# Three weight conversions, two bound matmuls and one split product set at other places in a three-layer kernel

## The chip, the core and the metric

The kernel runs on one core of one Trainium2 chip. The engines are TensorE (PE), VectorE (DVE), ScalarE (ACT), GpSimd (POOL) and SyncE (SP, which here only issues DMAs). The metric is the device time of one execution in microseconds. Before the change the median of 3 runs is 2321.61 us (2321.58 to 2321.97).

## The reference

The input is one sequence of 512 tokens with 1024 channels, in float32. It goes through an HGRN2 layer and a chunk-banded attention layer, each with a SwiGLU part, and then through a block in which half of the channels go to a two-directional mLSTM and half to a two-directional Hyena convolution, followed by an MLP. What is touched lies in that last block:

```python
hn = rms_norm_2(x, norm_mix_pre)
proj = (hn @ w_in).astype(f32)
cv = short_conv3(proj[..., :N_CONV], conv_w.astype(f32), conv_b.astype(f32))
q = heads(jax.nn.silu(cv[..., OFF_MQ:OFF_MQ + M_WIDTH]))
k = heads(jax.nn.silu(cv[..., OFF_MK:OFF_MK + M_WIDTH])) * (M_HEAD_DIM ** -0.5)
v = heads(proj[..., OFF_MV:OFF_MV + M_WIDTH])
o_gate = jax.nn.sigmoid(proj[..., OFF_MO:OFF_MO + M_WIDTH])
...
h_fwd = mlstm_chunkwise(q, k, v, gates[:, 0], jax.nn.log_sigmoid(gates[:, 1]))
h_bwd = flip(mlstm_chunkwise(flip(q), flip(k), flip(v), flip(gates[:, 2]), ...))
...
z = cv[..., OFF_HV:OFF_HV + H_WIDTH]
z = cv[..., OFF_HX1:...] * two_sided_fft_conv(z, filt[:, 0, 0], filt[:, 1, 0], fb[0])
z = cv[..., OFF_HX2:...] * two_sided_fft_conv(z, filt[:, 0, 1], filt[:, 1, 1], fb[1])
```

The mLSTM has 4 heads of 128 channels and, in the kernel, is computed without chunks: the 512 x 512 matrix of weights of each head and direction, exp(-max(bound - column, 0)), times the scores of queries and keys.

## The kernel before, in words

**Precision and weights.** Almost every matmul is three matmuls, from a high and a low half of each operand (`three`, L679 to L682). Weights come in slots of 128 x 2048 floats by DMA into one of 3 `raw` buffers. ACT copies a slot to its high half, `w_hi` (L1373, in `feed`), and DVE subtracts to get its low half, `w_lo` (L1847, also in a `feed`). There are 2 such pairs, used in turn. ACT and DVE are each one queue that is run in the order in which the program is written, and each calls `ahead(label, i)` at chosen places: it converts every slot up to the one behind (label, i) that isn't converted yet. So a call that is taken away puts its slot to the next call behind it. PE waits at the head of a slot for its `w_lo` (`weights`).

**Gates and mqk.** PE works through the slots mgate, mqk 0 to 3 (queries and keys, two chunks of 128 channels each), mv 0 and 1 (values), mo 0 and 1 (output gates), h2 0 to 5. In the loop over the four slots of mqk, DVE scales PE's result out of its bank (`scaled_conv`, L2258), ACT takes the middle tap of the convolution (L1650), DVE the outer ones (L2272, L2273), ACT the SiLU (L1655). Into slot i = 1 of that loop the gates are put: DVE copies their rows (L2299, L2300) and takes absolute values (L2301, releases `mg_q`), ACT takes the exponential (L1671) and the logarithm (L1673, releases `mg_l`), and in i = 2 and 3 DVE computes running sums and running maxima (L2304 to L2313). The first slot of mv claims all four rotating banks, which the chunks before must have left.

**mLSTM.** For each head h and direction d, PE spreads the bound over the partitions (`bound`, L1121; heads 2 and 3 use bank 0), DVE takes the differences (`exponents`, L2329, releases `ml_a`), ACT the exponential (`weights_of`, L1679), POOL masks four diagonal blocks (`mask_of`, L636), PE computes the scores (L1166), DVE multiplies (`masked`, L2341, releases `ml_p`), PE multiplies by the values (L1187; first the forward direction, then the backward one, four matmuls each, of which each makes two instructions), POOL sums the blocks (L650 to L658), PE sums over partitions (L1203), DVE inverts (L2359 to L2361) and puts the result on diagonals (L1890), PE spreads it (L1209), DVE combines (L2368 to L2370). `fill(n)` puts n steps of the output gates' matmuls between.

**Hyena.** For each of two orders o, PE transforms forward by a cosine and a sine table (eight outputs, `FORWARD`), DVE multiplies the spectra in four frequency blocks f (six operations each, L2421 to L2427, into buffers that alternate by f), ACT takes the high halves of the product (`upper_product`, L1740), DVE the low ones (`lower_product`, two L1861 for each f, release `u_l`), and PE transforms back (`back`): four groups of three matmuls for each block k of the cosine part, k = 0, 1, 2, then k = 0, 1 of the sine part, then the rest. `back` of block k waits for the low half of product k.

## Time and profile before

| what | value |
|---|---|
| median of 3 runs | 2321.61 us |
| the profiled execution's own time | 2321.61 us |
| its span | 2319.6 us |
| its mean granted clock of TensorE | 0.975 of full speed |
| PE busy | 2189.9 us, 94% |
| DVE busy | 1410.4 us, 61% |
| ACT busy | 752.1 us, 32% |
| POOL busy | 424.3 us, 18% |

The span runs from the first to the last instruction of the profiled execution; its own time is 2.0 us more. A busy share counts the time in which an engine had at least one instruction at work; matmuls overlap, so a busy PE is not PE at its peak. In a timeline each row gives the start in microseconds from the span's beginning, the duration, the engine, the line of the kernel, the operation with its output and inputs, how many like it stand in a row, and in brackets how long the engine had been idle and who ended that.

### The profile page before, as it was taken

The numbers are of one execution on the slowest core, as the hardware profiler recorded it, in microseconds if no ns is written. First come the engines' busy times: TensorE is split into PE (matmuls) and PEld (weight loads), VectorE is DVE, ScalarE is ACT, GpSimd is POOL, SyncE is SP. The second block draws the span as 40 slices with busy tenths as digits, with TensorE's granted clock in tenths as the row PEclk, the third lists the DMA queues.
The fourth block names the chain that finished last, engine by engine and source line by source line (L and its number), as shares of the span: only waits on it lengthen the run. The fifth ranks groups of instructions, "written<-read, shape, count | busy, mean of one in ns | idle before, by whom it ended". The sixth has DMA issues, their size and how long they took to land.

```text
span 2319.6 us, 25720 instructions
## 1 busy us (share of the span) xinstructions
PE 2189.9 (94%) x10094; PEld 1752.1 (76%) x10094; DVE 1410.4 (61%) x1929; ACT 752.1 (32%) x961; POOL 424.3 (18%) x272
## 2 busy tenths in 40 slices
PE   7899999979999997999989999998999998999997
PEld 5588788767888886866678888876568876888885
DVE  5666766554767767177455444467565776655656
ACT  1443334332222223256432222244233333322321
POOL 0000000039998873200000000000420000000000
PEclk9999999989999998999999999999999998999998
DMA  6343231225555542422122322322112221323220
GB/s 245 124 161 109 92 127 57 71 84 188 200 182 182 182 163 94 143 91 74 52 76 91 99 101 91 109 94 69 41 48 98 92 81 65 109 91 109 91 91 37
DMA packets 39327, 249.54 MB, mean 108 GB/s; under 512 B 4627, under 2 KB 4819, under 8 KB 11112
## 3 DMA queue, kind: packets, MB, share of 16 engines
q1 hardware_dynamic: 32856, 230.97, 28.7%
q0 software_dynamic: 3008, 10.63, 1.4%
q10 hardware_dynamic: 3344, 6.29, 0.7%
q8 instruction: 82, 1.34, 0.2%
q14 instruction: 37, 0.30, 0.0%
HBM read 241.58 MB, written 6.29 MB: 107 GB/s over the span
## 4 chain that ended last, share of the span: by engine, by line
PE 81%; DVE 8%; issue 4%; POOL 3%; ACT 2%; DMA 1%; SPq 0%; ACTq 0%; DVEq 0%; POOLq 0%
PE bank L680 24%; PE bank L682 23%; PE bank L681 23%; PE bank L907 2%; DVE w_lo L1847 2%; PE bank L727 1%; ACT w_hi L1373 1%; PE bank L1025 1%; PE bank L1035 1%; PE bank L1046 1%; POOL raw L593 1%; PE bank L714 1%; DMA raw<-in_wts 1%; PE bank L823 1%; POOL raw L594 1%
## 5 line engine op out<-in xcount | busy, mean ns | idle before, releaser
L680 PE MATMUL bank<-u_hi,w_hi 128*128 128x512 f32 x1708 | 695.1, 407 | 40.3 <-DVE w_lo L1847 11.8
L682 PE MATMUL bank<-u_hi,w_lo 128*128 128x512 f32 x1708 | 672.9, 394 | 0.0
L681 PE MATMUL bank<-u_lo,w_hi 128*128 128x512 f32 x1708 | 672.8, 394 | 0.0
L1847 DVE TENSOR_TENSOR w_lo<-raw,w_hi 128x2048 fp32r<-128x2048 f32 x162 | 427.8, 2641 | 225.9 <-ACT w_hi L1373 225.8
L680 PEld LDWEIGHTS bank<-u_hi,w_hi 128*128 128x128 f32 x1708 | 325.8, 191 | 129.6 <-issue 49.0
L1373 ACT ACTIVATE w_hi<-raw 128x2048 fp32r<-128x2048 f32 x162 | 309.1, 1908 | 341.6 <-PE bank L682 300.4
L682 PEld LDWEIGHTS bank<-u_hi,w_lo 128*128 128x128 f32 x1708 | 325.0, 190 | 70.0
L681 PEld LDWEIGHTS bank<-u_lo,w_hi 128*128 128x128 f32 x1708 | 326.1, 191 | 67.0 <-issue 3.8
L680 PE MATMUL bank<-g_hi,w_hi 128*128 128x512 f32 x772 | 306.2, 397 | 13.8 <-DVE w_lo L1847 6.4
L681 PE MATMUL bank<-g_lo,w_hi 128*128 128x512 f32 x772 | 301.8, 391 | 0.0
L682 PE MATMUL bank<-g_hi,w_lo 128*128 128x512 f32 x772 | 301.7, 391 | 0.0
L593 POOL TENSOR_TENSOR raw<-raw,cact 128x2048 f32<-128x2048 f32 x36 | 132.8, 3690 | 556.3 <-DVE u_lo L1913 483.3
L1935 DVE SCALAR_TENSOR_TENSOR H<-bank,modc,H 128x512 f32<-128x512 f32 x192 | 138.3, 745 | 84.7 <-PE bank L682 83.8
L680 PEld LDWEIGHTS bank<-g_hi,w_hi 128*128 128x128 f32 x772 | 145.7, 189 | 53.3 <-DVE w_lo L1847 8.2
L682 PEld LDWEIGHTS bank<-g_hi,w_lo 128*128 128x128 f32 x772 | 145.6, 189 | 30.9
L681 PEld LDWEIGHTS bank<-g_lo,w_hi 128*128 128x128 f32 x772 | 145.8, 189 | 29.0
L1549 ACT ACTIVATE pool<-bank 128x512 f32<-128x512 f32 x44 | 26.3, 599 | 314.8 <-PE bank L682 314.8
L594 POOL TENSOR_TENSOR raw<-raw 128x1024 f32<-128x1024 f32 x36 | 125.0, 3473 | 2.8
L2116 DVE TENSOR_TENSOR pool<-pool,bank 128x512 f32<-128x512 f32 x44 | 30.2, 687 | 154.8 <-ACT pool L1549 147.8
L1865 DVE TENSOR_TENSOR g_lo<-pool,g_hi 128x512 fp32r<-128x512 f32 x96 | 104.0, 1090 | 0.2
L2530 DVE TENSOR_TENSOR pool<-pool,bank 128x512 f32<-128x512 f32 x120 | 80.6, 684 | 23.6 <-PE bank L682 23.3
L626 POOL DMA_DIRECT2D pool<-in_tri x1 | 0.5, 536 | 453.2 <-DVE H L1935 453.2
(284 smaller groups left out, 2262.0 us busy)
## 6 DMA issues: line engine op xcount, KB each, us to landing
raw<-in_wts SPq DMA_DIRECT2D x218, 1024.0 KB, 4.8
spectra<-pool ACTq DMA_DIRECT2D x16, 256.0 KB, 2.0
scr<-in_rel POOLq DMA_DIRECT2D x16, 256.0 KB, 3.4
pool<-spectra POOLq DMA_DIRECT2D x16, 256.0 KB, 3.0
H<-in_x ACTq DMA_DIRECT2D x1, 2048.0 KB, 21.3
out<-H SPq DMA_DIRECT2D x8, 256.0 KB, 2.0
pool<-in_window POOLq DMA_DIRECT2D x1, 1024.0 KB, 9.1
pool<-in_filt_w POOLq DMA_DIRECT2D x1, 512.0 KB, 6.2
```

Of the source, the lines that this page charges most:

```text
L593: link(pl.tensor_tensor(chunks, chunks, cact[:, :].unsqueeze(2).broadcast_to((P, KC, 256)), ALU.mult))
L594: link(pl.tensor_tensor(src[:, 0:1024], src[:, 0:1024], src[:, 1024:2048], ALU.add))
L680: pe.matmul(out, lh, rh, start=start, stop=False, skip_group_check=True)
L681: pe.matmul(out, lh, rl, start=False, stop=False, skip_group_check=True)
L682: return pe.matmul(out, ll, rh, start=False, stop=stop, skip_group_check=True)
L907: mm = pe.matmul(b[:, t * P:(t + 1) * P], k[:, t * P:(t + 1) * P], q[:, t * P:(t + 1) * P], start=True, stop=True)
L1373: act.activation(w_hi[RING[w]][:, :], raw[s % raw_ring][:, :], ACT.Copy).then_inc(hi_done, 1)
L1847: dve.tensor_tensor(w_lo[RING[w]][:, :], raw[W_STREAM[w] % raw_ring][:, :], w_hi[RING[w]][:, :].bitcast(F32), ALU.subtract).then_inc(lo_do ...
L1865: dve.tensor_tensor(g_lo[:, n % NG, :], src, g_hi[:, n % NG, :].bitcast(F32), ALU.subtract).then_inc(g_l, 1)
L1935: dve.scalar_tensor_tensor(H[:, c, :], b[:, :], mcol(gate, c), H[:, c, :], ALU.mult, ALU.add).then_inc(free["dve"], 1)
L2116: dve.tensor_tensor(ff_h[:, i % 2, :], ff_s[:, i % 2, :], read(n + 1)[:, :], ALU.mult).then_inc(free["dve"], 1)
L2530: dve.tensor_tensor(Facc[:, c, :], Facc[:, c, :], b[:, :], ALU.add).then_inc(free["dve"], 1)
```

## The change

It has five places. In the mLSTM, `bound(h+1, 1)` for heads 2 and 3, with its wait, goes from ahead of both directions of L1187 to between them. In the loop over mqk, `ahead("mqk", 2)` is taken out of i = 1 on ACT and on DVE, which leaves slot mqk 3 to the same call at the start of i = 2. On DVE `ahead("mo", 1)`, which converts the first slot of h2, goes from head 2, behind `masked(3)`, to the end of head 1's round. In the hyena part `lower_product(2)` goes from ahead of the operations of f = 3 to behind them.

```diff
--- before.py
+++ after.py
@@ -1171,15 +1171,15 @@
             head_scores(0)
             fill(2)
             for h in range(M_HEADS):
-                if 2 <= h + 1 < M_HEADS:
-                    pe.wait_ge(ml_a, 2 * (h + 1) + 1)
-                    bound(h + 1, 1)
                 pe.wait_ge(ml_p, 8 * (h + 1))
                 if h:
                     pe.wait_ge(ml_nev, 2 * h)
                 else:
                     pe.wait_ge(ml_a, 2)
                 for d in range(2):
+                    if d and 2 <= h + 1 < M_HEADS:
+                        pe.wait_ge(ml_a, 2 * (h + 1) + 1)
+                        bound(h + 1, 1)
                     order = range(TB) if d == 0 else range(TB - 1, -1, -1)
                     for i in order:
                         a, z = (i * P, SEQ) if d == 0 else (0, (i + 1) * P)
@@ -1666,7 +1666,6 @@
                     act.wait_ge(*free_of(FIRST["mgate"]))
                     act.activation(g_all, g_all, ACT.Identity, bias=vcol("b_gates")).then_inc(mg_b, 1)
                 if i == 1:
-                    ahead("mqk", 2)
                     act.wait_ge(mg_q, 1)
                     act.activation(gt[0:M_HEADS], gt[0:M_HEADS], ACT.Exp, scale=-1.0).then_inc(mg_e, 1)
                     act.wait_ge(mg_e, 1)
@@ -2293,7 +2292,6 @@
                 for c in (2 * i, 2 * i + 1):
                     update_H(c)
                 if i == 1:
-                    ahead("mqk", 2)
                     dve.wait_ge(mg_b, 1)
                     for d in range(2):
                         dve.tensor_copy(gi[0:M_HEADS, d, :], g_all[64 * d:64 * d + M_HEADS, :])
@@ -2353,8 +2351,6 @@
                 if h + 1 < M_HEADS:
                     masked(h + 1)
                     scaled_out(FIRST["mo"] + h, m_og[:, h, :])
-                if h == 2:
-                    ahead("mo", 1)
                 dve.wait_ge(ml_den, h + 1)
                 link(dve.tensor_tensor(m_dd[:, 0:8], bank[6][:, 0:8], em[:, :, h], ALU.max))
                 link(dve.scalar_tensor_tensor(m_dd[:, 0:8], bank[6][:, 0:8], -1.0, m_dd[:, 0:8], ALU.mult, ALU.max))
@@ -2370,6 +2366,8 @@
                 dve.tensor_tensor(m_h[:, h, :], m_h[:, h, :], scr[:, 3, :], ALU.add).then_inc(ml_h, 1)
                 if h + 2 < M_HEADS:
                     exponents(h + 2, 1)
+                if h == 1:
+                    ahead("mo", 1)
             scaled_out(FIRST["mo"] + M_HEADS - 1, m_og[:, M_HEADS - 1, :])
             ahead("h2", 0)
             dve.wait_ge(ml_h, M_HEADS)
@@ -2408,7 +2406,6 @@
                 for f in range(4):
                     e = 4 * o + f
                     if f == 3:
-                        lower_product(2)
                         ahead("dft", 2 * o + 1)
                     if f >= 2:
                         dve.wait_ge(u_l, U_Y[o] + 2 * (f - 1))
@@ -2431,7 +2428,7 @@
                         ins = dve.tensor_copy(ys[0:1, :], bb[0:1, :])
                     ins.then_inc(hy_y, 1)
                     dve.wait_ge(hy_y, e + 1)
-                    if f in (1, 2):
+                    if f:
                         lower_product(f - 1)
                 lower_product(3)
                 if o:
```

What this does to the queues is seen at three places. On ACT, in the loop over mqk, the high half of slot mqk 3 (L1373) stands ahead of the exponential and the logarithm of the gates (L1671, L1673) before:

```order
L1655 ACTIVATE pool<-pool 128x512 x2
L1373 ACTIVATE w_hi<-raw 128x2048
L1671 ACT_TABLE_LOAD
L1671 ACTIVATE scr<-scr 4x1024
L1673 ACT_TABLE_LOAD
L1673 ACTIVATE scr<-scr,onec 4x1024
L1650 ACTIVATE pool<-macc,vec 128x512 x2
L1655 ACT_TABLE_LOAD
```

and now (where those two are L1670 and L1672):

```order
L1655 ACTIVATE pool<-pool 128x512 x2
L1670 ACT_TABLE_LOAD
L1670 ACTIVATE scr<-scr 4x1024
L1672 ACT_TABLE_LOAD
L1672 ACTIVATE scr<-scr,onec 4x1024
L1373 ACTIVATE w_hi<-raw 128x2048
L1650 ACTIVATE pool<-macc,vec 128x512 x2
L1655 ACT_TABLE_LOAD
```

The same slot's low half moves in the same way on DVE, from ahead of the gate rows to behind them.

On DVE, in the mLSTM, from the last `exponents` (L2329) of head 3 over `masked(3)` (L2341) to the inversion (L2359), before:

```order
L2329 TENSOR_SCALAR pool<-bank,pool 128x512
L2341 SCALAR_TENSOR_TENSOR pool<-bank,pool 128x512
L2341 SCALAR_TENSOR_TENSOR pool<-bank,pool 128x128
L2341 SCALAR_TENSOR_TENSOR pool<-bank,pool 128x384
L2341 SCALAR_TENSOR_TENSOR pool<-bank,pool 128x256 x2
L2341 SCALAR_TENSOR_TENSOR pool<-bank,pool 128x384
L2341 SCALAR_TENSOR_TENSOR pool<-bank,pool 128x128
L2341 SCALAR_TENSOR_TENSOR pool<-bank,pool 128x512
L2258 TENSOR_TENSOR pool<-bank,macc 128x512
L1847 TENSOR_TENSOR w_lo<-raw,w_hi 128x2048
L2359 TENSOR_TENSOR pool<-bank,pool 128x8
L2360 SCALAR_TENSOR_TENSOR pool<-bank,pool 128x8
```

and now (`exponents` is L2327, `masked` L2339, the inversion L2355 and L2356, `w_lo` L1846):

```order
L2327 TENSOR_SCALAR pool<-bank,pool 128x512
L1846 TENSOR_TENSOR w_lo<-raw,w_hi 128x2048
L2339 SCALAR_TENSOR_TENSOR pool<-bank,pool 128x512
L2339 SCALAR_TENSOR_TENSOR pool<-bank,pool 128x128
L2339 SCALAR_TENSOR_TENSOR pool<-bank,pool 128x384
L2339 SCALAR_TENSOR_TENSOR pool<-bank,pool 128x256 x2
L2339 SCALAR_TENSOR_TENSOR pool<-bank,pool 128x384
L2339 SCALAR_TENSOR_TENSOR pool<-bank,pool 128x128
L2339 SCALAR_TENSOR_TENSOR pool<-bank,pool 128x512
L2257 TENSOR_TENSOR pool<-bank,macc 128x512
L2355 TENSOR_TENSOR pool<-bank,pool 128x8
L2356 SCALAR_TENSOR_TENSOR pool<-bank,pool 128x8
```

The conversion of h2's first slot has moved from behind the seven rows of `masked(3)` and the scaled gate to ahead of them.

On DVE, in the first hyena pass, the rows from the last of f = 2 to the last `lower_product` (L1861), before:

```order
L2427 TENSOR_TENSOR scr<-scr 128x512
L1861 TENSOR_TENSOR u_lo<-scr,u_hi 128x512 x4
L1847 TENSOR_TENSOR w_lo<-raw,w_hi 128x2048
L2421 TENSOR_TENSOR scr<-pool 128x512
L2422 TENSOR_TENSOR scr<-bank,pool 128x512
L2423 TENSOR_TENSOR scr<-pool 128x512
L2424 TENSOR_TENSOR scr<-bank,pool 128x512
L2426 TENSOR_TENSOR scr<-scr 128x512
L2427 TENSOR_TENSOR scr<-scr 128x512
L1861 TENSOR_TENSOR u_lo<-scr,u_hi 128x512 x2
```

and now (L1860, with the six operations as L2418 to L2424):

```order
L2424 TENSOR_TENSOR scr<-scr 128x512
L1860 TENSOR_TENSOR u_lo<-scr,u_hi 128x512 x2
L1846 TENSOR_TENSOR w_lo<-raw,w_hi 128x2048
L2418 TENSOR_TENSOR scr<-pool 128x512
L2419 TENSOR_TENSOR scr<-bank,pool 128x512
L2420 TENSOR_TENSOR scr<-pool 128x512
L2421 TENSOR_TENSOR scr<-bank,pool 128x512
L2423 TENSOR_TENSOR scr<-scr 128x512
L2424 TENSOR_TENSOR scr<-scr 128x512
L1860 TENSOR_TENSOR u_lo<-scr,u_hi 128x512 x4
```

Two of the four low halves ahead of `w_lo` now stand behind the six operations of f = 3. The second pass changes in the same way.

## Rows read from the trace of the kernel before

**Rows 1.** The page, part 1: engine, busy us, share of the span, instructions.

```profile
PE 2189.9 (94%) x10094; PEld 1752.1 (76%) x10094; DVE 1410.4 (61%) x1929; ACT 752.1 (32%) x961; POOL 424.3 (18%) x272
```

**Rows 2.** Timeline of PE (start, us, engine, line, operation, idle before), after four waits.

```profile
435.63 0.77 PE L680 MATMUL bank<-u_hi,w_hi 128*128 128x512 f32 x1 [3.23 <-DVE u_lo L1861]
...
1149.55 0.50 PE L680 MATMUL bank<-g_hi,w_hi 128*128 128x512 f32 x1 [2.92 <-DVE w_lo L1847]
...
1589.98 0.50 PE L680 MATMUL bank<-u_hi,w_hi 128*128 128x512 f32 x1 [1.70 <-DVE w_lo L1847]
...
1608.64 0.77 PE L680 MATMUL bank<-w_hi,u_hi 128*128 128x512 f32 x1 [7.44 <-DVE macc L2258]
```

**Rows 3.** Timeline of ACT, gates.

```profile
1585.70 1.90 ACT L1373 ACTIVATE w_hi<-raw 128x2048 fp32r<-128x2048 f32 x1
...
1595.22 1.15 ACT L1673 ACTIVATE scr<-scr,onec 4x1024 f32<-4x1024 f32 x1
```

**Rows 4.** Timeline of DVE, gates.

```profile
1587.63 2.29 DVE L1847 TENSOR_TENSOR w_lo<-raw,w_hi 128x2048 fp32r<-128x2048 f32 x1 [1.19 <-ACT w_hi L1373]
...
1591.59 1.21 DVE L2301 SCALAR_TENSOR_TENSOR scr<-scr 4x1024 f32<-4x1024 f32 x1
...
1597.17 0.75 DVE L2272 SCALAR_TENSOR_TENSOR pool<-macc,vec,pool 128x511 f32<-128x511 f32 x1 [3.17 <-ACT pool L1650]
...
1605.00 2.29 DVE L1847 TENSOR_TENSOR w_lo<-raw,w_hi 128x2048 fp32r<-128x2048 f32 x1
...
1607.21 1.28 DVE L2258 TENSOR_TENSOR macc<-bank,macc 128x512 f32<-128x512 f32 x2
```

**Rows 5.** Timeline of DVE, heads 2 and 3 of the mLSTM.

```profile
1687.68 1.91 DVE L2329 TENSOR_SCALAR pool<-bank,pool 128x128 f32<-128x128 f32 x4
...
1694.85 1.68 DVE L2341 SCALAR_TENSOR_TENSOR pool<-bank,pool 128x512 f32<-128x512 f32 x4 [5.25 <-POOL pool L636]
...
1699.90 2.28 DVE L1847 TENSOR_TENSOR w_lo<-raw,w_hi 128x2048 fp32r<-128x2048 f32 x1
...
1702.10 0.16 DVE L2359 TENSOR_TENSOR pool<-bank,pool 128x8 f32<-128x8 f32 x1
```

**Rows 6.** Timeline of DVE, both hyena passes.

```profile
1819.16 2.50 DVE L1861 TENSOR_TENSOR u_lo<-scr,u_hi 128x512 fp32r<-128x512 f32 x4
...
1827.49 0.69 DVE L2427 TENSOR_TENSOR scr<-scr 128x512 f32<-128x512 f32 x1
...
1871.51 0.68 DVE L2427 TENSOR_TENSOR scr<-scr 128x512 f32<-128x512 f32 x1
```

**Rows 7.** Timeline of PE, third input block of both backward passes.

```profile
1824.23 0.39 PE L680 MATMUL bank<-u_hi,w_hi 128*128 128x512 f32 x1
...
1868.23 0.39 PE L680 MATMUL bank<-u_hi,w_hi 128*128 128x512 f32 x1
```

**Rows 8.** Timeline of PE, heads 2 and 3.

```profile
1683.47 1.88 PE L1209 MATMUL bank<-scr,ones 128*128 128x512 f32 x4
...
1686.34 4.58 PE L1187 MATMUL bank<-pool 128*128 128x512 f32 x16
...
1698.99 1.84 PE L1203 MATMUL bank<-onec,scr 128*128 128x1 f32 x16
...
1703.90 2.26 PE L1209 MATMUL bank<-scr,ones 128*128 128x512 f32 x4 [0.19 <-DVE scr L1890]
```

**Rows 9.** Timeline of ACT and of POOL, head 3.

```profile
1690.81 1.90 ACT L1373 ACTIVATE w_hi<-raw 128x2048 fp32r<-128x2048 f32 x1
...
1693.11 1.71 POOL L636 TENSOR_TENSOR pool<-pool 128x128 f32<-128x128 f32 x4
```

**Rows 10.** Stretches of PE: from:to us, length, busy (instructions), granted clock, DMA share, GB/s.

```profile
435.60:441.00 5.40, 5.37 (x13) 0.50 0.01 3
...
1608.60:1612.00 3.40, 3.36 (x8) 0.50 0.64 270
```

**Rows 11.** The line L636 of POOL: count, ns least/median/most, first and last start.

```profile
L636 POOL TENSOR_TENSOR pool<-pool x32: 449/458/2512, 1628.6 to 1694.4; 128x128 f32<-128x128 f32 x32
```

## The prediction

> **What bounds the kernel now.** I read the busy shares first: PE is busy 94% of the span [rows 1], so a wait costs time only where PE has nothing else to issue, or where it ends last for PE. Then I read the timelines of PE, DVE, ACT and POOL at the three places that the diff touches, looking for PE's idle time and for what ended it.
>
> - The gates (1585 to 1622 us). PE stands 1.70 us before the last slot of mqk, for its w_lo, and 7.44 us before the first slot of mv, for DVE's L2258 (`scaled_conv` of channel 7, which frees a bank) [rows 2]. DVE is the late one there, and DVE waited 3.17 us for ACT, which was at the exponential and the logarithm [rows 3, 4].
> - The mLSTM heads (1640 to 1716 us). PE, DVE and POOL hand each head on; before head 3's `masked`, DVE stands 5.25 us until POOL's L636 [rows 5], and that is the chain.
> - The two hyena passes (1805 to 1885 us). PE streams without a gap, and DVE delivers the low halves just ahead of it [rows 6, 7].
>
> **The change, part by part.** Times are those of before; a later place is shifted by what the earlier ones add.
>
> *1. Bounds.* `bound(h+1,1)` for heads 2 and 3 goes behind the four forward matmuls of L1187, half of 4.58 us [rows 8], so about 2.2 us later; PE issues the same work, and its wait on ml_a was already met. DVE's exponents of (3,1) start about 0.9 us later than 1687.68, and ACT's w_hi behind them at 1691.7 instead of 1690.81 [rows 5, 9]. Alone this is hidden: in before w_hi is wanted only at 1699.90 [rows 5]. Alone I put it at 0, between -0.2 and +0.9 (what DVE loses, if something waited for it). With part 3 the 0.9 us is no longer covered.
>
> *2. The last slot of mqk.* ACT's w_hi and DVE's w_lo now stand behind the gate rows. DVE goes into them at 1586.4 (1.19 us idle before 1587.63 [rows 4]). They took from the end of w_lo, about 1589.9, to 1592.8 (1591.59 + 1.21), 2.9 us: now done at 1589.3. From there to the end of the logarithm it took 1596.37 - 1592.80 = 3.57 us [rows 3, 4]: now 1592.9. Then w_hi, 1.90 us [rows 3], to 1594.8, then w_lo, 2.29 us, to about 1597.1. PE starts the slot there instead of at 1589.98, standing 8.8 us instead of 1.70. Much is paid back. The slot took 11.2 us at full clock (1589.98 to 1608.64 - 7.44). After 8.8 us of rest the clock will be at its 1.2 GHz level, as it was after 7.44 us (granted 0.50 from 1608.6 to 1612 [rows 10]); the slow stretch costs half its length, 1.7 us there (3.4 us) and 2.7 us after a rest of 3.23 us (5.4 us [rows 2, 10]); I take 2.2, the middle. PE ends the slot at 1597.1 + 11.2 + 2.2 = 1610.5, L2258 of channel 7 follows in 0.7 us (two take 1.28 [rows 4]), and mv starts at 1611.2. The conversion for it is not late: DVE's taps start at 1597.1 + 1.28 for the two L2258 and some 0.4 for ACT's middle tap (my allowance), so at 1598.8 instead of 1597.17, and w_lo moves from 1605.00 to 1606.6 and ends by 1608.9 [rows 4]. Before, mv started at 1608.64 with a slow stretch of its own worth 1.7; now the rest is under 1 us and it runs at full clock. Net 1611.2 - (1608.64 + 1.7) = +0.9 us. Bounds: +0.4 and +1.4 with 1.7 and 2.7, and +2.6 if mv starts slow all the same.
>
> *3. The first slot of h2.* w_lo leaves the place before L2359 at head 2, where PE's column sums were done about 1700.8 and DVE came at 1702.10 [rows 5, 8]: at most 1.3 us of DVE. It goes ahead of `masked(3)`. ACT's w_hi ends at 1691.7 + 1.90 = 1693.6, and w_lo runs 1693.7 to about 1696.0; in before `masked(3)` began at 1694.85. Worse, POOL's four L636 of head 3 stand at 1693.11 to 1694.82 [rows 9], and `masked(3)` needs them. An L636 takes 0.46 us and in one case 2.51 [rows 11], the one that met a w_lo. So after two of them POOL stands until 1696.1, two more end at 1697.1, and `masked(3)` starts 2.3 us late. PE's column sums move from 1698.99 to 1701.3; four gate steps behind them fill 2.9 us, and L1209 comes at 1705.8 instead of 1703.90. Before, L1209 also waited between its pairs and ended at 1706.2 (2.26 us for four, where free ones take 1.88 [rows 8]); now 1705.8 + 1.9 = 1707.7. Net +1.5 us. Bounds: +2.3 if all of the delay is passed on, and -0.7 if w_lo were hidden (four gate steps after 1700.7 end at 1703.6, and 1703.6 + 1.9 stands against 1706.2); only DVE's own 1.1 us late gives +0.4.
>
> The Trainium skill, "SBUF — State Buffer", section on SBUF's two separate sides, says that the pair of ports shared by VectorE and GpSimd is locked for a whole instruction, so that the loser fully blocks. By that rule the late start is the full 2.3 us, without it 1.1; the trace agrees (2.51 us [rows 11]).
>
> *4. Hyena.* `lower_product(2)` goes behind the six operations of f = 3 in both passes. In before it was inside the four L1861 at 1819.16 [rows 6], and PE took up its third input block, the ninth group of three, at 1824.23 (1868.23 in the second pass) [rows 7], 2.6 us after. w_lo of the table gains nothing, since it waits for ACT's w_hi and starts at 1822.15 as before. So f = 3 ends when it did: 1827.49 + 0.69 = 1828.18, and 1871.51 + 0.68 = 1872.19 in the second pass [rows 6]. Then one L1861, 0.69 us, and PE's third block starts at 1828.95 and 1872.95, so PE stands 4.7 us per pass. It has nothing else to issue: `back` takes the blocks in order, and the groups behind it are queued. Nothing gives this back, because from here on PE ends last: DVE stood idle before the output rows of each pass. In stalls: 9.4 us. A rest of 4.7 us lies above the one of 3.23 us after which the clock was at its lower level, and above the 2.92 us after which it was not (first matmul 0.77 against 0.50) [rows 2]. So I take a fall in each pass, 2.2 us each (bounds 0 and 2.7). Sum 2 x (4.7 + 2.2) = 13.8; bounds 9.4 and 14.8.
>
> Sum: 0 + 0.9 + 1.5 + 13.8 = +16.2 us. The profiled execution took 2321.61 us with a span of 2319.6; its own time is the median of the three runs. So 2337.8 us, span 2335.8.
>
> **The rivals.**
>
> *B. The clock holds in the hyena stalls.* For it: the stall begins out of dense work, as the one of 2.92 us did; against it, the rest of 3.23 us. It gives 0.9 + 1.5 + 9.4 = +11.8, 2333.4 us; with a fall in one pass alone 2335.6. The Trainium skill, "TensorE: Matmul & The Clock Gate", Part 1, says that the chip's view of PE's activity runs free of the program, so that the point of change differs from run to run; by that a stall of this length can pass without a fall, which is this rival, 0.25.
>
> *C. The postponed product is not waited for*, because PE comes to the third block later than the trace shows. Then only parts 2 and 3 count, +2.4, 2324.0. Against it: both passes show PE there 4.7 us too early, and nothing moved shifts PE against DVE inside a pass. 0.04.
>
> *D. Faster.* The exponential and the logarithm start 1592.8 - 1589.3 = 3.5 us earlier, and the 7.44 us before mv hang on them. If PE got its mqk weights in time, mv would start 3.5 us earlier, -3.5. It decides only if ACT could convert between the exponential's wait and its start; in the new order w_hi stands behind the logarithm on ACT. It also needs C; with part 3's best case 2321.6 - 3.5 - 0.7 = 2317.4. 0.03.
>
> *E. More is lost*: mv starts slow (+1.7), all of part 3 is passed on (+0.8), and the slow stretches are long (+1.0): 2341.3. 0.08.
>
> **How the numbers follow.** The forecast, 2337.8 with its own range 2335 to 2340.5, gets 0.60, B 0.25, E 0.08, C 0.04, D 0.03. The range of 2331 to 2341.5 takes in B and E. A measurement of this kernel can tell 0.2% from no change, 4.6 us: forecast, B and E lie above it, 0.93; C is within, 0.04; D is 4.2 us faster, on the edge of it, and the chance of a gain beyond that is 0.03.
>
> **What would show it.** PE idle about 8.8 us before the last mqk slot and under 1 us before mv; two new waits of PE of 4.7 us for L1861 (now L1860) in the backward passes, each with granted clock at 0.5 behind it; `masked(3)` behind a w_lo, with one L636 over 2 us; the same instruction counts. It is wrong if PE does not wait in the backward passes, or if the total there is under 9 us; if the clock holds, the time falls by 2.2 us per pass.

## The result and the profile after

The changed kernel takes 2347.86 us (median of 4 runs, 2342.69 to 2348.81), the kernel before beside it 2321.6 us (2321.33 to 2321.97). The ratio is 1.0104, with an interval of 1.0090 to 1.0118: slower by 1.0%. The profiled execution took 2343.47 us with a span of 2341.5 and a mean granted clock of 0.969; before it was 2321.61 us and 0.975. So the traces show 21.9 us of the loss, and it is these that are taken apart here. Repeated on another occasion, the changed kernel had a median of 2342.96 us against 2322.84, ratio 1.0084 [1.0071, 1.0097]; both intervals hold 0.90 to 0.97%.

Timeline of PE, the gates, after (start, us, engine, line, operation, idle before), as in [rows 2]:

```profile
1597.23 0.79 PE L680 MATMUL bank<-u_hi,w_hi 128*128 128x512 f32 x1 [8.78 <-DVE w_lo L1846]
...
1611.69 0.47 PE L680 MATMUL bank<-w_hi,u_hi 128*128 128x512 f32 x1 [0.95 <-DVE macc L2257]
```

Timeline of ACT and DVE there, as in [rows 3, 4]:

```profile
1591.91 1.15 ACT L1672 ACTIVATE scr<-scr,onec 4x1024 f32<-4x1024 f32 x1
1592.96 1.89 ACT L1373 ACTIVATE w_hi<-raw 128x2048 fp32r<-128x2048 f32 x1
1594.89 2.29 DVE L1846 TENSOR_TENSOR w_lo<-raw,w_hi 128x2048 fp32r<-128x2048 f32 x1 [5.38 <-ACT w_hi L1373]
```

The wait has moved from in front of mv (7.44 us before) to in front of the last mqk slot (8.78 us, before 1.70). The two waits add up to 9.73 us where there were 9.14, and the exponential and the logarithm are indeed earlier, but `w_hi` has to stand behind them.

Timeline of POOL, DVE and PE at head 3, as in [rows 5, 8, 9]:

```profile
1694.58 3.76 POOL L636 TENSOR_TENSOR pool<-pool 128x128 f32<-128x128 f32 x4
```

```profile
1695.03 2.59 DVE L1846 TENSOR_TENSOR w_lo<-raw,w_hi 128x2048 fp32r<-128x2048 f32 x1 [3.14 <-ACT w_hi L1373]
1698.37 1.69 DVE L2339 SCALAR_TENSOR_TENSOR pool<-bank,pool 128x512 f32<-128x512 f32 x4 [0.76 <-POOL pool L636]
...
1706.97 0.17 DVE L2355 TENSOR_TENSOR pool<-bank,pool 128x8 f32<-128x8 f32 x1 [0.99 <-PE bank L1203]
```

```profile
1699.32 2.08 PE L1166 MATMUL bank<-pool 128*128 128x512 f32 x2 [3.92 <-DVE pool L2339]
1700.40 1.42 PE L680 MATMUL bank<-u_hi,w_hi 128*128 128x512 f32 x1
1701.62 0.63 PE L681 MATMUL bank<-u_lo,w_hi 128*128 128x512 f32 x1
```

POOL's four L636 take 3.76 us instead of 1.71 with `w_lo` running beside them, `masked(3)` starts behind them, and PE waits 3.92 us before the third L1166. The matmul behind it (L681) takes 0.63 us, which is what one takes at half clock; at full clock it is 0.39. Before, PE waited 1.75 us there and the matmul took 0.39 (timeline of PE, before):

```profile
1695.79 1.12 PE L1166 MATMUL bank<-pool 128*128 128x512 f32 x2 [1.75 <-DVE pool L2341]
...
1696.99 0.39 PE L681 MATMUL bank<-u_lo,w_hi 128*128 128x512 f32 x1
```

Timeline of PE and DVE in the hyena passes, as in [rows 6, 7]; the PE rows are the third input block of both passes:

```profile
1835.89 0.80 PE L680 MATMUL bank<-u_hi,w_hi 128*128 128x512 f32 x1 [4.57 <-DVE u_lo L1860]
...
1887.20 0.80 PE L680 MATMUL bank<-u_hi,w_hi 128*128 128x512 f32 x1 [4.58 <-DVE u_lo L1860]
```

```profile
1834.42 0.68 DVE L2424 TENSOR_TENSOR scr<-scr 128x512 f32<-128x512 f32 x1
1835.14 2.50 DVE L1860 TENSOR_TENSOR u_lo<-scr,u_hi 128x512 fp32r<-128x512 f32 x4
```

These two waits did not exist before: PE took the same block up without idle time [rows 7]. Stretches of all engines after (from:to, length, busy of each engine, granted clock, DMA share, GB/s), as in [rows 10]:

```profile
1835.90:1841.50 5.60, 5.60 (x14) 4.39 (x15) 1.74 (x3) 0.39 (x1) 0.57 (x2) 0.53 0.31 94
1887.20:1892.80 5.60, 5.60 (x14) 4.44 (x15) 4.16 (x7) 2.49 (x5) 0.00 (x0) 0.54 0.00 0
1699.30:1702.70 3.40, 3.38 (x6) 2.06 (x7) 1.65 (x4) 0.00 (x0) 0.00 (x0) 0.50 0.65 275
1736.00:1740.00 4.00, 4.00 (x14) 3.42 (x14) 3.31 (x7) 2.08 (x2) 0.00 (x0) 0.50 0.00 0
```

The clock is at its 1.2 GHz level behind both hyena waits, behind the wait of head 3, and once more 37 us later at 1736, where PE had not waited at all. The last stretch has a smaller fellow in the kernel before:

```profile
1732.00:1736.00 4.00, 4.00 (x13) 0.64 0.00 0
```

### The profile page after: what moved, and what is told of

The parts are those of the page before. It is cut to its first block, busy times and chain, and to the rows that moved or that the text cites. A ratio compares the mean times of both kernels' runs of the same rounds, so it can differ in the third digit from the quotient of the medians.

```text
span 2341.5 us, 25720 instructions
## 1 busy us (share of the span) xinstructions
PE 2200.5 (94%) x10094; PEld 1760.6 (75%) x10094; DVE 1411.5 (60%) x1929; ACT 752.0 (32%) x961; POOL 424.6 (18%) x272
## 4 chain that ended last, share of the span: by engine, by line
PE 80%; DVE 9%; issue 5%; POOL 3%; ACT 2%; DMA 1%; SPq 0%; ACTq 0%; DVEq 0%; POOLq 0%
PE bank L680 23%; PE bank L682 22%; PE bank L681 22%; PE bank L907 2%; DVE w_lo L1846 2%; PE bank L727 1%; ACT w_hi L1373 1%; PE bank L1025 1%; PE bank L1035 1%; PE bank L1046 1%; POOL raw L593 1%; PE bank L714 1%; DMA raw<-in_wts 1%; PE bank L823 1%; POOL raw L594 1%
## 5 line engine op out<-in xcount | busy, mean ns | idle before, releaser
L681 PE MATMUL bank<-u_lo,w_hi 128*128 128x512 f32 x1708 | 676.5, 396 | 0.0
L1846 DVE TENSOR_TENSOR w_lo<-raw,w_hi 128x2048 fp32r<-128x2048 f32 x162 | 427.8, 2641 | 237.6 <-ACT w_hi L1373 237.5
L1373 ACT ACTIVATE w_hi<-raw 128x2048 fp32r<-128x2048 f32 x162 | 309.1, 1908 | 348.4 <-PE bank L682 306.9
L681 PEld LDWEIGHTS bank<-u_lo,w_hi 128*128 128x128 f32 x1708 | 328.5, 192 | 67.7 <-issue 4.4
L681 PE MATMUL bank<-g_lo,w_hi 128*128 128x512 f32 x772 | 302.0, 391 | 0.0
L681 PEld LDWEIGHTS bank<-g_lo,w_hi 128*128 128x128 f32 x772 | 145.8, 189 | 29.0
L1549 ACT ACTIVATE pool<-bank 128x512 f32<-128x512 f32 x44 | 26.3, 597 | 315.2 <-PE bank L682 315.2
```

The source lines that it names most:

```text
L681: pe.matmul(out, lh, rl, start=False, stop=False, skip_group_check=True)
L1373: act.activation(w_hi[RING[w]][:, :], raw[s % raw_ring][:, :], ACT.Copy).then_inc(hi_done, 1)
L1846: dve.tensor_tensor(w_lo[RING[w]][:, :], raw[W_STREAM[w] % raw_ring][:, :], w_hi[RING[w]][:, :].bitcast(F32), ALU.subtract).then_inc(lo_do ...
```

## How the loss is divided

Some places can be found in the trace of each kernel of this study, so each stage can be measured by itself: **gates**, from the first matmul of mgate (1551.77 in before) to the first transpose of the values (L1114); **heads**, from the wait of 0.87 us for head 0's scores to DVE's inversion for head 2 (L2359); **E-F**, from there to the first transpose L1218 with 0.79 us idle, ahead of the hyena passes; **passes**, from there to the wait of 1.39 us behind them. Lengths in us, each from one profiled execution; the last column is what lies ahead of the first place, which no edit touches. The 18.2 us between gates and heads are the same in all kernels.

| kernel | gates | heads | E-F | passes | ahead |
|---|---|---|---|---|---|
| before | 69.53 | 62.56 | 99.86 | 89.58 | 1551.77 |
| after | 70.82 | 65.96 | 101.91 | 104.20 | 1551.96 |
| p1_bounds | 69.51 | 62.49 | 99.86 | 89.56 | 1552.10 |
| p2_gates | 71.95 | 62.67 | 101.46 | 89.56 | 1554.82 |
| p3_mo | 69.55 | 64.84 | 100.28 | 89.56 | 1552.66 |
| q2_mo_wait | 69.54 | 66.50 | 101.92 | 89.52 | 1550.92 |
| p4_hyena | 70.64 | 64.19 | 98.24 | 103.72 | 1555.49 |
| q1_hyena_fill | 69.70 | 62.64 | 99.85 | 99.25 | 1551.83 |
| q3_gates_dve | 65.95 | 62.57 | 98.28 | 89.52 | 1551.10 |
| q4_best | 64.57 | 61.25 | 101.90 | 89.52 | 1556.74 |
| r1_after | 70.67 | 65.86 | 101.94 | 104.11 | 1552.60 |
| r2_after_mo_fill | 70.83 | 63.42 | 98.69 | 103.39 | 1553.79 |
| r3_after_both_fill | 70.69 | 63.33 | 98.69 | 99.35 | 1552.56 |
| r4_after_no_mo | 71.90 | 64.21 | 99.84 | 104.16 | 1550.63 |

After against before: +1.29 gates, +3.40 heads, +2.05 E-F, +14.62 passes, and +0.19 ahead and +0.36 behind, where the code is the same. That is 21.9 us.

Three columns tell how far one execution can be trusted. Ahead of the first place, identical code takes 1550.6 to 1556.7 us. The gates stage took 1.1 us more in p4_hyena, which doesn't touch it: there the clock fell behind the wait of 2.33 us at the head of the stage, and it did the same in p2_gates, q3_gates_dve and r4_after_no_mo, but not in the other ten. Stretches of PE, the 3 us behind that wait in before and in p2_gates:

```profile
1551.77:1554.77 3.00, 3.00 (x13) 1.00 0.67 199
```

```profile
1554.82:1557.82 3.00, 3.00 (x7) 0.50 0.69 208
```

And E-F takes 98.2 to 101.9 us. The stretch with the slow clock, 88 to 104 us behind head 0's scores, is what makes most of the difference. It is as long in q4_best and in p2_gates, where PE waits 1.76 and 1.89 us at head 3, as in after, r1 and q2, where it waits 3.9 to 4.1; it is shorter in before, p1, p3, q1 and r4; and it is missing in p4_hyena and q3_gates_dve, whose waits are left as they are, as well as in r2 and r3, where the wait is filled. Stretches of PE in r1_after, q4_best and q3_gates_dve:

```profile
1731.50:1743.50 12.00, 12.00 (x57) 0.72 0.01 2
```

```profile
1729.55:1741.55 12.00, 12.00 (x43) 0.72 0.26 87
```

```profile
1725.28:1737.28 12.00, 12.00 (x61) 1.00 0.26 87
```

So most of the +2.05 us of E-F can't be put down to an edit. A stage that one execution shows 1 to 3 us longer proves nothing by itself; the rows in it have to show why.

## The experiments

All ratios are to the kernel before, timed beside them, with 95% intervals.

**p1_bounds: the bounds alone.**

```diff
-                if 2 <= h + 1 < M_HEADS:
-                    pe.wait_ge(ml_a, 2 * (h + 1) + 1)
-                    bound(h + 1, 1)
...
                 for d in range(2):
+                    if d and 2 <= h + 1 < M_HEADS:
+                        pe.wait_ge(ml_a, 2 * (h + 1) + 1)
+                        bound(h + 1, 1)
```

> The move of the two bounds alone. Theory A (each part costs what its own wait costs): 0 us, between -0.2 and +0.3, since the w_hi behind it on ACT is wanted only 9 us later. Rival: the 0.9 us that DVE's exponents lose is passed on to PE, +0.9 us. PE's wait before the third L1166 stays near 1.75 us by theory A.

2322.02 us (2320.62 to 2325.32, 11 runs) against 2324.37, ratio 0.9992 [0.9983, 1.0000]. All stages within 0.1 us of before: it costs nothing.

**p2_gates: the slot of mqk alone, on ACT and DVE.**

```diff
                 if i == 1:
-                    ahead("mqk", 2)
                     act.wait_ge(mg_q, 1)
...
                 if i == 1:
-                    ahead("mqk", 2)
                     dve.wait_ge(mg_b, 1)
```

> The moved conversion of slot mqk 3 alone, on ACT and DVE. Theory A: +1.3 us, as the changed kernel's trace shows at this place (8.78 us of wait before the slot, 0.95 before mv, against 1.70 and 7.44), and one slow stretch as before, only earlier. Rival: the spread of 6 us between executions of the changed kernel (2342.7 to 2348.8) comes from here; then some executions of this one stand 5 us above the others.

2325.65 us (2322.90 to 2329.33), ratio 1.0009 [1.0001, 1.0018]. The gates stage is 2.42 us longer here. In the other five kernels that hold the same edit it is 1.14 to 1.30 us longer (after, r1, r2, r3) and 2.37 (r4). The 1.1 us more in p2_gates and r4 are not the edit's: in both the clock fell behind the wait at the head of the stage, ahead of every edit, as in p4_hyena, which took 1.1 us more without the edit. So the edit costs 1.1 to 1.3 us, as expected, which is less than the spread of the totals. The rival isn't borne out: the executions spread by 6.4 us here, and those of before beside them by no less.

**p3_mo: the first slot of h2 alone.**

```diff
-                if h == 2:
-                    ahead("mo", 1)
                 dve.wait_ge(ml_den, h + 1)
...
                 if h + 2 < M_HEADS:
                     exponents(h + 2, 1)
+                if h == 1:
+                    ahead("mo", 1)
```

> The moved conversion of h2's first slot alone, without the moved bounds. w_hi on ACT ends 0.9 us earlier than in the changed kernel, and w_lo meets POOL's four L636 from their start. Theory A (w_lo blocks L636, so masked(3) starts about 2.3 us late, and the clock falls in the longer wait): one L636 above 2 us, PE's wait before the third L1166 3 to 4 us instead of 1.75, time +3 to +5.5 us. Rival (the clock does not matter here, only the late start does): +1.5 us. If the time is above that by 3 us and the granted clock behind the wait is 0.5, theory A stands.

2326.59 us (2324.02 to 2330.09), ratio 1.0014 [1.0005, 1.0023], 1.2 to 5.3 us; by medians 2.2, which is under the 3 to 5.5 expected and doesn't by itself exclude the rival's 1.5. The trace decides: in the 3.4 us behind the wait the granted clock is 0.56, and heads is 2.28 us longer and E-F 0.42. Timelines of POOL and PE:

```profile
1694.04 3.74 POOL L636 TENSOR_TENSOR pool<-pool 128x128 f32<-128x128 f32 x4
```

```profile
1698.76 2.08 PE L1166 MATMUL bank<-pool 128*128 128x512 f32 x2 [3.80 <-DVE pool L2341]
```

The blocked POOL and the longer wait are there without any other edit. So part 3 alone makes them, and doesn't need the later bounds.

**p4_hyena: the hyena passes alone.**

```diff
                     if f == 3:
-                        lower_product(2)
                         ahead("dft", 2 * o + 1)
...
-                    if f in (1, 2):
+                    if f:
                         lower_product(f - 1)
```

> The moved product alone. Theory A: two waits of 4.6 us of PE for the low half and a slow stretch behind each, worth 2.6 to 2.9 us: +14.4 us, 2336.0. Rival (the clock holds without the stalls ahead of it): +9.2 us, 2330.8. If the 6 us of spread belong here, some executions are 5 us longer than others.

2338.40 us (2334.37 to 2345.25), ratio 1.0065 [1.0049, 1.0080]. The passes take 14.14 us more, where 14.4 were expected. Heads and E-F together come out as before (162.43 from the scores of head 0 on, against 162.42), but by chance: heads has a slow stretch more and E-F one less. This one edit is two thirds of the loss.

The four parts add up: -0.08 + 0.09 + 0.14 + 0.65 = +0.80%, against 0.84% and 1.04% for all of them together. The intervals of the four leave about 0.2% open in that sum, so an interplay of less than some 5 us would not be seen.

**q1_hyena_fill: p4_hyena with 16 matmuls, whose results nobody uses, ahead of the third block of each backward pass.**

```diff
                 for k in range(3):
+                    if k == 2:
+                        pe.wait_ge(*free_of(FIRST[f"fb{o}_2"]))
+                        for x in range(16):
+                            pe.matmul(bank[PLACE[FIRST[f"fb{o}_2"]]][:, :], hi_c[:, 0:P], u_hi[:, 0, :], start=True, stop=True)
                     for j in range(4):
                         back(hi_c, lo_c, 0, k, j)
```

> The moved product alone, with 16 dummy matmuls of PE (128x128 by 128x512, 0.23 us each, 3.6 us in all, into a bank that is free) put ahead of the third block of each backward pass; their results are not used. Theory A (a stall costs its own length and a slow stretch of the clock behind it): the stall is still there in wall time (3.6 us of dummies and about 1 us of idle), but the granted clock stays at 1.0, so the place costs 9.2 us instead of 14.1, and the whole about 2331. Rival (the 5 us beyond the stalls have another cause, such as a later DVE): the place costs 14 us again, though the clock stays up.

2335.29 us (2331.94 to 2336.77) against 2324.04, ratio 1.0048 [1.0036, 1.0060]. Timeline of PE, first pass:

```profile
1824.53 3.79 PE L1275 MATMUL bank<-u_hi,w_hi 128*128 128x512 f32 x16
...
1829.25 0.50 PE L680 MATMUL bank<-u_hi,w_hi 128*128 128x512 f32 x1 [0.94 <-DVE u_lo L1865]
1829.59 0.39 PE L681 MATMUL bank<-u_lo,w_hi 128*128 128x512 f32 x1
```

PE is as late as in p4_hyena, since the wait is for DVE, but the matmuls behind it take 0.39 us: the clock has held. The passes cost 9.67 us more than before instead of 14.14. So 4.5 us, 2.2 for each pass, are the clock's. Of the 9.7 us that stay, the two waits are 2 x 4.58 = 9.2; the other 0.5 us are assigned to nothing. The expected 2331 us lies 4 us under the median; the expected 9.2 us for the place nearly came.

**q2_mo_wait: p1_bounds and p3_mo, and DVE waits until all of head 3's masks are done before it converts.**

```diff
                 if h == 1:
+                    dve.wait_ge(ml_m, 8)
                     ahead("mo", 1)
```

> The moved bounds and the moved conversion of h2's first slot, but DVE waits for POOL's masks of head 3 before it converts. Theory A (w_lo blocks POOL, and the mask is late): every L636 is below 0.6 us but the first ones of the stage, masks end about 1.9 us earlier than with the conversion first; but w_lo now stands behind the masks, so masked(3) starts 2.3 us late all the same, the wait before the third L1166 is again near 4 us, and the time is like the one with the conversion first, +2 to +3 us. Rival (the wait for ACT's w_hi is what makes masked(3) late, not the block): w_lo would start after 1695 and the wait be over 4.5 us.

2326.72 us (2323.72 to 2333.20), ratio 1.0018 [1.0006, 1.0029], by medians 2.7 us above before, as expected. Timelines of POOL, DVE and PE:

```profile
1692.28 1.70 POOL L636 TENSOR_TENSOR pool<-pool 128x128 f32<-128x128 f32 x4
```

```profile
1694.02 2.29 DVE L1847 TENSOR_TENSOR w_lo<-raw,w_hi 128x2048 fp32r<-128x2048 f32 x1 [4.45 <-POOL pool L636]
1696.23 1.67 DVE L2341 SCALAR_TENSOR_TENSOR pool<-bank,pool 128x512 f32<-128x512 f32 x4
```

```profile
1697.16 2.08 PE L1166 MATMUL bank<-pool 128*128 128x512 f32 x2 [4.08 <-DVE pool L2341]
```

POOL isn't blocked any more, and `masked(3)` starts no earlier: `w_lo` stands before it in the queue either way. Counted from head 0's scores it starts 2.2 us later than in before, and 2.1 in after. So the late start comes with the order in DVE's queue; who is blocked only says where the same 2 us appear. The rival's wait of over 4.5 us didn't come: it is 4.08, and `w_lo` starts behind POOL's masks and not behind ACT.

**q3_gates_dve: only DVE's half of the slot of mqk is moved, ACT's high half stays where it was.**

```diff
@@ DVE
                 if i == 1:
-                    ahead("mqk", 2)
                     dve.wait_ge(mg_b, 1)
```

> Only DVE's conversion of slot mqk 3 moved behind the gate rows; ACT converts ahead of the exponential as before. Theory A (the 7.44 us before mv hang on ACT's exponential and logarithm, which start when DVE has done the gate rows, and w_hi fits into ACT's wait for them): PE waits about 3.3 us before the last mqk slot (1.70 before) and under 1 us before mv, mv starts about 5 us earlier, and time falls by 5 to 6.5 us (the clock falls in one of the two waits or in none). Rival (the wait before mv is for PE's own bank, freed late whatever the gates do): mv starts within 1 us of before, and time is the same or 1.6 us longer.

2318.36 us (2315.51 to 2321.91, 11 runs), ratio 0.9979 [0.9971, 0.9988]: faster than before, by about 5 us, as expected. Timelines of ACT, DVE and PE:

```profile
1586.52 1.90 ACT L1373 ACTIVATE w_hi<-raw 128x2048 fp32r<-128x2048 f32 x1
...
1590.18 1.06 ACT L1671 ACTIVATE scr<-scr 4x1024 f32<-4x1024 f32 x1 [0.46 <-DVE scr L2300]
```

```profile
1590.08 2.27 DVE L1847 TENSOR_TENSOR w_lo<-raw,w_hi 128x2048 fp32r<-128x2048 f32 x1
```

```profile
1592.40 0.79 PE L680 MATMUL bank<-u_hi,w_hi 128*128 128x512 f32 x1 [3.30 <-DVE w_lo L1847]
```

ACT would only have waited for the gate rows (2.26 us in after), so its `w_hi` is free there; DVE's `w_lo` is what kept the gate rows back. PE's wait before the slot is 3.30 us instead of 8.78, and 1.05 before mv. The stage is 3.58 us shorter, although the clock fell at its head in this execution; in q4_best, which has the same edit and where it held there, the stage is 4.96 us shorter.

**q4_best: q3_gates_dve, and the first slot of h2 behind head 2's last combination.**

```diff
+                if h == 2:
+                    ahead("mo", 1)
```

(at the end of the round, in place of the one ahead of the inversion, beside the edit of q3_gates_dve)

> As the kernel with DVE's conversion alone moved, and the conversion of h2's first slot put behind head 2's last combination (L2370) on DVE, where DVE stood idle 3.8 us before. Theory A: L2359 of head 2 comes 1.3 us earlier, PE's L1209 waits no more between its pairs, 0.7 to 0.9 us less than the kernel with DVE's conversion alone; in all -6 to -7.5 us. Rival (DVE's early start there is lost to POOL's sums, which share its ports): no difference from that kernel.

2320.33 us (2314.89 to 2323.50), ratio 0.9984 [0.9975, 0.9993]. The span to DVE's inversion is another 1.3 us shorter than in q3_gates_dve (61.25 against 62.57), but the times don't show it: the median is 3.7 us below before instead of the expected 6 to 7.5, and the intervals of the two overlap. In its trace the slow stretch of E-F takes more than that 1.3 us back, so whether the earlier inversion is worth anything stays open. q3_gates_dve stays the best version that was run.

**r1_after: the changed kernel again**, as the ground for the three below.

> The changed kernel once more, beside the kernel before on the same chip, as the ground for the three others. Theory (the loss is in two waits that it makes longer and in the slow clock behind them): its median lies 20 to 26 us above the kernel before; before the third score product of head 3 TensorE waits 3.9 us where it waited 1.75, and the granted clock in the 4 us behind that wait is under 0.8. Rival (the slow clock in that place was an accident of the one profiled execution, the loss there is 2.1 us): the clock there is above 0.95.

2342.96 us (2341.41 to 2345.35), ratio 1.0084 [1.0071, 1.0097], 20.1 us above before. In the trace the wait is 3.92 us again, and the clock behind it 0.50 (stretch of PE):

```profile
1699.80:1703.80 4.00, 4.00 (x7) 0.50 0.53 223
```

**r2_after_mo_fill: 14 unused matmuls in the wait before head 3's third score product.**

```diff
                     if n >= 2:
+                        if n == 14:
+                            pe.wait_ge(ml_h, 2)
+                            for x in range(14):
+                                pe.matmul(bank[7][:, :], u_hi[:, 0, 0:P], u_hi[:, 0, :], start=True, stop=True)
                         pe.wait_ge(ml_p, 2 * (n - 1))
```

> The changed kernel with 14 matmuls of 128x512 whose results nobody uses, put ahead of the third score product of head 3, where TensorE waits 3.9 us. They take 14 x 0.23 = 3.2 us, so the wait stays where it ends and TensorE works through most of it. Theory (the wait of 3.9 us lets the clock fall, and this is what the prediction missed in the conversion that was moved ahead of the masks): the product still starts 2.1 us late, but the granted clock behind it stays at 1.00, so that the inversion of head 2's denominators lies at most 2.3 us behind the kernel before instead of 3.4. Median 1.5 to 3 us below the changed kernel. Rival (the clock falls whatever TensorE does, in stretches of its own time): clock and times are as in the changed kernel.

2337.08 us (2334.25 to 2340.38, 6 runs), ratio 1.0058 [1.0046, 1.0069]: 5.9 us below r1_after. Timeline and stretch of PE:

```profile
1697.19 3.36 PE L1168 MATMUL bank<-u_hi 128*128 128x512 f32 x14
1701.17 1.13 PE L1170 MATMUL bank<-pool 128*128 128x512 f32 x2 [0.62 <-DVE pool L2343]
1701.73 0.79 PE L680 MATMUL bank<-u_hi,w_hi 128*128 128x512 f32 x1
1702.36 0.40 PE L681 MATMUL bank<-u_lo,w_hi 128*128 128x512 f32 x1
```

```profile
1701.10:1704.50 3.40, 3.33 (x12) 1.00 0.69 277
```

The score product starts exactly as long after head 0's scores as in r1_after (58.32 and 58.30 us), but the clock is at its 2.4 GHz level. Heads is 2.44 us shorter: that is the clock's share behind this wait. E-F is 3.25 us shorter, because the slow stretch at 1732 to 1744 isn't there either; but it is missing in p4_hyena and q3_gates_dve too, which fill nothing, so no run shows that the filled wait took it away. The medians give twice the 1.5 to 3 us expected, with an uncertainty of about 4 us.

**r3_after_both_fill: r2_after_mo_fill and the 16 matmuls of q1_hyena_fill.**

> The changed kernel with the 14 unused matmuls of the run ahead and 16 more ahead of the third block of each of the two backward passes (4.6 us of wait each). Theory: both slow stretches of the hyena passes and the one of head 3 go, the waits stay: 6 to 8 us below the changed kernel by medians, that is 14 to 17 us above the kernel before: 9.2 for the two hyena waits, 2.1 for head 3, 1 for the gates. Rival (all of the loss is the waits, the clock costs nothing because other work would have waited anyway): no more than 1 us below the changed kernel.

2332.56 us (2331.51 to 2333.88), ratio 1.0039 [1.0027, 1.0051]: 10.4 us below r1_after, where 6 to 8 were expected. By the traces 2.5 us of it lie in heads and 4.8 in the passes, behind the filled waits, and 3.25 in E-F, where the cause is open. Stretches of PE behind the two hyena waits:

```profile
1830.50:1836.00 5.50, 5.49 (x24) 1.00 0.30 98
1879.40:1885.00 5.60, 5.60 (x25) 1.00 0.00 0
```

24 instructions in 5.5 us where there were 14 in 5.6. Of the whole loss of 20.1 us, 7.3 are thus shown to be the clock behind the three waits; by medians, with the stretch in E-F, it is half.

**r4_after_no_mo: the changed kernel with part 3 undone** (the edit of p3_mo taken back).

> The changed kernel with part 3 undone: the first slot of the output conversion is behind head 3's masks again. Theory (part 3 costs 3 to 5 us in company of the others): 3 to 5 us below the changed kernel, and in the trace the third score product of head 3 waits 1.75 us and the clock behind it holds. Rival (part 3 costs the 1.5 us of the prediction): 1.5 us below. Second rival (what is late at head 3 is caught up later): the same time as the changed kernel.

2341.92 us (2339.34 to 2344.19, 5 runs), ratio 1.0078 [1.0066, 1.0090]. By medians that is 1.0 us below r1_after, less than the 3 to 5 expected; the intervals overlap. By the traces, from head 0's scores to L1218 it takes 164.05 us, where r1_after takes 167.80, so 3.75 less, and the gates stage took 1.2 more. The row shows why so little comes back:

```profile
1697.01 1.98 PE L1166 MATMUL bank<-pool 128*128 128x512 f32 x2 [1.87 <-DVE pool L2339]
```

```profile
1697.00:1701.00 4.00, 3.99 (x8) 0.57 0.00 0
```

In this execution the clock fell after a wait of only 1.87 us. It held after 1.75 to 1.89 us in before, p1, p2, q1, q3 and q4, fell for a part of the time in p4 (1.89 us), and fell behind all four waits of 3.8 to 4.1 us (after, r1, q2, and for some 3 us in p3). So the short wait here may be followed by a fall, 2 times in 8, and the long one was each time. Of the 3.75 us less, 1.65 lie in heads and 2.10 in E-F. What part 3 costs in company is therefore known only as between about 1 (medians) and 5.5 us (traces), and alone 1.2 to 5.3.

## Why the prediction was wrong

**Sign and order of the parts** were right: slower, with the hyena passes as the largest term, the head next, the gates small and the bounds nothing. The forecast was 16.2 us, the profiled execution shows 21.9, and the median 26.3.

- *Part 1, bounds: 0.* Right (p1_bounds, every stage within 0.1 us).
- *Part 2, gates: +0.9.* The steps came as worked out: PE's slot at 1597.2 (forecast 1597.1), mv at 1611.7 (1611.2), the waits 8.78 and 0.95. It cost +1.3. The +2.4 of p2_gates and r4 holds 1.1 us from a slow stretch ahead of the edit, which the prediction's bounds weren't about.
- *Part 3, first slot of h2: +1.5. This is the step that failed.* The late start was right: `masked(3)` 2.1 us later (forecast 2.3), POOL blocked in one L636 (2.51 us again, below), the score product 2.1 us later. The prediction then went on from there with full-clock durations ("four gate steps behind them fill 2.9 us"). But the late start stretches PE's own wait before the third L1166 from 1.75 to 3.92 us, longer than the 3.23 us after which the clock had been seen at its lower level [rows 2]. The rule was used for the hyena waits and for the gates in the same text, and forgotten here. The clock behind this wait, put at nothing, took 65.96 - 63.42 = 2.5 us (after against r2_after_mo_fill, where the wait is filled). The late start by itself was priced well: r2 and q3_gates_dve have no slow stretch between head 0's scores and L1218, and take 162.11 and 160.85 us, so it costs +1.3 with the clock held (forecast +1.5). Part 3 thus cost 1.3 + 2.5 = 3.8 us at its place. The stretch shows 167.87 - 162.42 = 5.45; the other 1.65 is the slow stretch near 1736, 3.2 us of loss in after and 1.6 in before, which no run ties to part 3.

The line L636 after (count, ns least/median/most), which answers to [rows 11]:

```profile
L636 POOL TENSOR_TENSOR pool<-pool x32: 448/458/2509, 1630.1 to 1697.9; 128x128 f32<-128x128 f32 x32
```

- *Part 4, hyena: +13.8.* 14.6 measured. The stall per pass was 4.57 us (forecast 4.7); behind it another (14.6 - 9.2) / 2 = 2.7 us were lost in each pass of after, 2.5 in p4_hyena, where 2.2 had been taken and 2.7 was the bound. q1_hyena_fill and r3_after_both_fill show that it was the wait that brought the clock down, since the matmuls that fill it keep it up; they give back 2.2 and 2.4 us for each pass, so some 0.3 us of each 2.5 to 2.7 is not the clock.
- *Rivals.* B (the clock holds) didn't come in any of the ten hyena waits of after, p4, r1, r2 and r4. Its chance of 0.25 was too high: the trace of before alone has other waits that speak against it, of 2.96 us at 492 and 1182 and of more, each with 0.50 behind it. The 2.92 us at 1149.55 after which the clock held, one of the prediction's two marks, was one draw: the same wait has the clock below 1.00 behind it in seven of the 14 traces. C is refuted by the two waits of 4.57 and 4.58 us. D failed as a description of this change, yet its mechanism is real: q3_gates_dve leaves ACT's conversion inside its wait and gains 3.58 us in that stage, where D had 3.5 (and 4.96 in q4_best without the fall at its head, so the nearness of 3.58 is luck). E, with 2341.3, was the nearest; the loss lay in the place that it had right (head 3), for a reason that it didn't have.
- *The range.* It counted the unknown prices and not that one execution differs from the next. The forecast for the median is 10.1 us too low: 2.3 for part 3 at its place, 1.7 for the stretch near 1736, 0.8 hyena, 0.4 gates, 0.5 where the code is the same, and 4.4 by which the median lies above the profiled execution. So the failed step is the largest term that the traces show, and would alone have moved the forecast only to about 2340. The eight executions of the changed kernel lie between 2342.69 and 2348.81 us, with mean clocks of 0.970 down to 0.965, and the same kernel took 2341.41 to 2345.35 later. The stages ahead of every edit already differ by 6.1 us between the kernels. That can make 3 to 5 us of difference between two medians of a few runs. Which of this is chance and which a condition of the chip at that moment stays open.

## What to carry to other kernels

When an edit makes any wait of the busiest engine longer, price two things: the wait, and the clock behind it; here the second was between a third and a half of the whole loss (7.3 to 10.4 of 20.1 us), and a wait of 1.75 us that grew to 3.92 cost more by its clock (2.5 us) than by its length (1.3). Go through every wait on the path with the same table of "rest, clock after it", not only through those that the diff makes, and fill the table from more than two rows and, where there are several, from all traces. And a conversion in two halves on two engines need not be moved as a whole: leave the half of the engine that would wait anyway (ACT, at the gates), move the half of the one that is late (DVE): 0.2% faster than before, where moving both was slower.

## What the runs showed of the hardware that was not expected

- The same wait at the same place is followed by a slow stretch in one execution and not in the next. In the 14 traces, from 60 us on, the granted clock in the 2 us behind a wait was 0.50 for all 140 waits of 2.96 us or more. Below that it depends on the place and the execution: it was under 0.97 behind the 2.9 us at 1150 in 7 of 14, the 2.33 us at 1552 in 4, the 2.17 us at 998 in 5 and the 1.91 us at 246 in 11. Behind the 1.4 us at 1142 and the 1.39 at 1892 it held in all 28. This agrees with the Trainium skill, "TensorE: Matmul & The Clock Gate", Part 1, by which the chip's view of PE's activity runs free of the program.
- The granted clock can also fall with no wait close ahead of it. The stretch at 1732 to 1744 us has no idle time of PE in front of it from 1709 us on. It is long (0.72 over 12 us) in after, r1, q2, p2 and q4, shorter in before, p1, p3, q1 and r4, and missing in p4, q3, r2 and r3; p2 and p4 hold the code of before there, and took 101.46 and 98.24 us for E-F. So the slow stretches of a kernel aren't a fixed property of its program. What sets this one off stays open.
- A `w_lo` of DVE beside POOL's L636 delays both: the L636 that meets it takes 2.51 us instead of 0.46, and the `w_lo` 2.47 to 2.59 us instead of 2.29. Ordering the two (q2_mo_wait) restores both durations and gains nothing, because the next step stands behind both. The Trainium skill, "SBUF — State Buffer", section on SBUF's two separate sides, has the loser of the shared ports blocked for the whole instruction, and the one that starts first, DVE or POOL, is the winner. The trace agrees for POOL (2.51 - 0.46 = 2.05 us of a `w_lo` of 2.3); the 0.2 to 0.3 us that `w_lo` loses fit the other direction, since it starts while an L636 is at work.
